# RWKV and DeltaNet scans with split state products, an mLSTM scan of 36 units in one line, and norm heads that add squares first

## What is computed

```python
h = rms_norm(x, g) * (1.0 + scale) + shift            # a "norm head", four of them
# DeltaNet, one chunk (RWKV is alike, with decays per channel):
delta = u_c - einsum('bhtk,bhvk->bhtv', w_c, s)        # u_c, w_c: triangular solve
o = einsum('bhtk,bhvk->bhtv', qd, s) + einsum('bhti,bhiv->bhtv', a_c, delta)
s = gl * s + einsum('bhtv,bhtk->bhvk', delta, kd)
# mLSTM, one chunk:
w_intra = exp(log_intra - m_t); w_inter = exp(log_inter - m_t)
s = einsum('bhtk,bhik->bhti', q, k) * w_intra
num = w_inter * einsum('bhtk,bhvk->bhtv', q, c) + einsum('bhti,bhiv->bhtv', s, v)
den = w_inter * einsum('bhtk,bhk->bht', q, n) + sum(s, axis=-1)
h = num / maximum(abs(den), exp(-m_t))
c = w_inter[-1] * c + einsum('bhi,bhiv,bhik->bhvk', w_end, v, k)
```

## Time and profile before

| | us |
|---|---|
| median of 3 runs (5168.05 to 5174.02) | 5173.57 |
| the profiled execution | 5176.75 |
| its span | 5175.1 |
| around the span | 1.65 |

### The profile page before, as it was taken

How to read it: one execution, slowest core, us unless ns; L and a number is a source line. 1 busy time by engine, 2 the same in 40 slices (tenths; PEclk the granted TensorE clock), 3 DMA queues, 4 the chain that set the end, 5 groups by cost and what they waited for, 6 DMA issues and landing times. The chain is left out here.

```text
span 5175.1 us, 94331 instructions
## 1 busy us (share of the span) xinstructions
PE 4152.8 (80%) x37921; PEld 3731.0 (72%) x37921; DVE 2183.8 (42%) x3966; ACT 1040.0 (20%) x1645; POOL 959.2 (19%) x676
## 2 busy tenths in 40 slices
PE   5999676367776778367999999799387388999998
PEld 3999332156665667156999999799366287999998
DVE  1333335233333434243655555200555435564555
ACT  2100223512222333222200010201222303110001
POOL 3322000000000422022222222321011023212222
PEclk8999888689999888678999999999566588999999
DMA  3222465311111211210111111122132311111111
GB/s 121 69 93 81 156 207 176 140 52 52 52 52 36 83 54 43 99 60 25 37 48 41 45 37 37 51 86 72 45 90 85 118 33 37 41 40 46 44 41 61
DMA packets 439441, 360.28 MB, mean 70 GB/s; under 512 B 63220, under 2 KB 417709, under 8 KB 436621
## 3 DMA queue, kind: packets, MB, share of 16 engines
q1 hardware_dynamic: 406993, 272.91, 17.6%
q0 software_dynamic: 10304, 60.98, 2.9%
q10 hardware_dynamic: 21888, 22.55, 1.2%
HBM read 270.45 MB, written 85.92 MB: 69 GB/s over the span
## 5 line engine op out<-in xcount | busy, mean ns | idle before, releaser
L91 POOL TENSOR_TENSOR ffn_w_lower<-ffn_w,ffn_w_upper 128x1024 fp32r<-128x1024 f32 x168 | 402.7, 2397 | 1296.0 <-DVE ffn_w_upper L86 1296.0
L872 DVE SCALAR_TENSOR_TENSOR conv_acc<-u_tile,ffn_taps,conv_acc 128x945 f32<-128x945 f32 (+3 forms) x440 | 488.9, 1111 | 86.9 <-ACT conv_acc L830 72.9
L99 PE MATMUL ffn_ps<-HU,ffn_w_upper 128*128 128x384 f32 x2112 | 485.7, 337 | 47.8 <-POOL HL L91 47.7
L99 PE MATMUL ffn_ps<-HU,ffn_w_lower 128*128 128x384 f32 x2112 | 484.0, 337 | 0.0
L99 PE MATMUL ffn_ps<-HL,ffn_w_upper 128*128 128x384 f32 x2112 | 483.7, 337 | 0.0
L99 PEld LDWEIGHTS ffn_ps<-HU,ffn_w_upper 128*128 128x128 f32 x2112 | 378.3, 189 | 55.3 <-POOL HL L91 33.5
L99 PEld LDWEIGHTS ffn_ps<-HU,ffn_w_lower 128*128 128x128 f32 x2112 | 380.6, 190 | 0.0
L99 PEld LDWEIGHTS ffn_ps<-HL,ffn_w_upper 128*128 128x128 f32 x2112 | 380.1, 190 | 0.0
L99 PE MATMUL ffn_out_ps<-g_upper,ffn_w_upper 128*128 128x384 f32 x1056 | 355.3, 336 | 14.4 <-DVE g_lower L91 14.4
L99 PE MATMUL ffn_out_ps<-g_lower,ffn_w_upper 128*128 128x384 f32 x1056 | 354.8, 336 | 0.0
L99 PE MATMUL ffn_out_ps<-g_upper,ffn_w_lower 128*128 128x384 f32 x1056 | 354.8, 336 | 0.0
(11 more groups left out here) (461 smaller groups left out, 6910.5 us busy)
## 6 DMA issues: line engine op xcount, KB each, us to landing
ffn_w<-in_ffn_w_in_dram SPq DMA_DIRECT2D x88, 512.0 KB
ada_w<-in_ada_w_dram SPq DMA_DIRECT2D x40, 1024.0 KB, 6.4
rwkv_units<-unit_rows POOLq DMA_DIRECT2D x8, 2304.0 KB, 8.9
un<-rwkv_units SPq DMA_DIRECT2D x36, 512.0 KB, 4.6
z_even<-z_tile POOLq DMA_DIRECT2D x31, 576.0 KB, 3.1
in_w<-in_ab_w_in_dram SPq DMA_DIRECT2D x31, 512.0 KB
gun<-gdn_units SPq DMA_DIRECT2D x72, 192.0 KB, 3.8
z_odd<-z_tile POOLq DMA_DIRECT2D x24, 576.0 KB, 4.9
```

What stands on the lines that cost most here:

```text
L91: return eng.tensor_tensor(out.bitcast(F32R), x, up, ALU.subtract)
L99: mm = pe.matmul(o, w(a).bitcast(F32R), r.bitcast(F32R), start=(first and n == 0), stop=(last and n == 2))
L872: dve.scalar_tensor_tensor(out=o, in0=i, scalar=tp[:, t:t + 1], in1=o, op0=ALU.mult, op1=ALU.add).then_inc(s["conv"] if n < NCONV else s[" ...
```

## The change

Four parts.

- **Norm heads.** VectorE adds the eight squares into one tile (`added`), then PE sums once with six matmuls. Squares and scaled blocks have four buffers in place of two; VectorE scales block k before it cuts block k-1. In `ffn_phase` the four buffers lie in the memory that the products use later.
- **RWKV scan.** The first product y0 (16 matmuls) opens the slot (`first`), then the products and the transposes of tokens and keys. VectorE makes the level 0 matrices before the masks. Update, both output products and the right side are made in halves, one between x and dy and one after dy of levels 1 to 5 (`beside`). ScalarE's output copy moves behind level 3. SyncE's loads wait for out_carried in place of out_own.
- **DeltaNet scan.** SyncE starts the output stores. A half of out stands ahead of dy in levels 1 and 2, a half of update in levels 3 and 4; state steps come in quarters in levels 4 and 5; the exponentials come one per level.
- **mLSTM scan.** Context and latent steps form one list of 36 units without a loop, with two state tiles (`ml_ctx`, `ml_lat`); states are turned in before the list and out after it. A constant `never` (a large negative number above the diagonal) is added on VectorE in place of clipping and GpSimd's mask, and ScalarE's exponential takes the column as its bias. The state product follows inter at once, in other columns of PSUM. GpSimd makes h, SyncE starts the stores, columns are read in place.

```diff
-        if k >= 2:
-            act.wait_ge(s["summed"], k - 1)
-        act.activation(self.tmp[k % 2], self.XT[:, k, :], ACT.Square).then_inc(s["squared"], 1)
-    act.wait_ge(s["summed"], KD)
+        if k > n:
+            act.wait_ge(s["added"], k - n)
...
 def tensor(self, pe):
-    for k in range(KD):
-        pe.wait_ge(self.s["squared"], k + 1)
-        for b, i, j in BANKS:
-            mm = pe.matmul(self.ps[:, b, 0:j - i], self.ones[:], self.tmp[k % 2][:, i:j],
-               start=(k == 0), stop=(k == KD - 1))
-        mm.then_inc(self.s["summed"], 1)
+    pe.wait_ge(self.s["added"], KD - 1)
+    for b, i, j in BANKS:
+        mm = pe.matmul(self.ps[:, b, 0:j - i], self.ones[:], self.rstd[:, i:j], start=True, stop=True)
...
+    s, n = self.s, len(self.tmp)
     dve.memset(self.eps[:], RMS_EPS).then_inc(s["eps_set"], 1)
+    for k in range(1, KD):
+        dve.wait_ge(s["squared"], k + 1)
+        if k > 1:
+            dve.wait_ge(s["added"], k - 1)
+        dve.tensor_tensor(self.rstd[:], self.rstd[:], self.tmp[(k - 1) % n], ALU.add).then_inc(s["added"], 1)
...
     for k in range(KD):
-        if k >= 2:
-            cut(k - 2)
-            dve.wait_ge(s["n_lower"], k - 1)
-        scale(k, self.tmp[k % 2])
-    cut(KD - 2)
+        if k >= n:
+            dve.wait_ge(s["n_lower"], k - n + 1)
+        for h, (a, b) in enumerate(HALVES):
+            dve.scalar_tensor_tensor(out=self.tmp[k % n][:, a:b], in0=self.XT[:, k, a:b], scalar=self.gain[:, k, h:h + 1],
+                         in1=self.rstd[:, a:b], op0=ALU.mult, op1=ALU.mult).then_inc(s["scaled"], 1)
+        if k:
+            cut(k - 1)
     cut(KD - 1)
...
+        def beside(l, g):
+            if l == 4:
+                if g == 0:
+                    rhs_carried(new)
+            elif l == 5:
+                rhs_own(new, g)
+            elif old is not None:
+                (update, out_carried, out_own)[l - 1](old, g)
+        if new is None:
+            solve(old)
+            for stage in (update, out_carried, out_own):
+                for g in range(2):
+                    stage(old, g)
+            return
+        first(new)
+        for g in range(2):
+            products(new, g)
+        tokens(new)
         if old is not None:
             solve(old)
-        if new is None:
-            update(old)
-            out_carried(old)
-            out_own(old)
-            return
-        tokens(new)
-        for g in range(2):
-            products(new, g)
         k_tokens(new)
         for g in range(2):
             dv.wait(pe, f"{a + g}n1", it)
-            block_w(pe, ps, st, K, B, a + g, g, 0)
-        if old is not None:
-            update(old)
         ac.wait(pe, f"{a}kt1", it)
         for l in range(1, NL - 1):
             each(block_w, l)
-            if l == 1 and old is not None:
-                out_carried(old)
-            if l == 4:
-                rhs_carried(new)
             each(block_x, l)
-            if l == 1 and old is not None:
-                out_own(old)
-            if l == 4:
-                rhs_own(new)
+            beside(l, 0)
             each(block_dy, l)
+            beside(l, 1)
         for g in range(2):
             dv.wait(pe, f"{a + g}Y{NL - 2}", it)
...
+        levels(1, 2, 3)
         if old is not None:
             out()
-        levels(3, 4)
+        levels(4, 5)
...
+                                         K["pairs0"][:, None, :, :].to_broadcast([P, 2, 2, RL]), ALU.mult), f"{a}Z{h}")
+            dv.wait(dve, f"{a}Z1", it)
+            for g in range(2):
+                dv.did(dve.tensor_tensor(Y[:, g], K["ident64"][:, None, :].to_broadcast([P, 4, RL]), W[:, g],
+                                         ALU.subtract), f"{a + g}Y0")
             for g in range(2):
                 q = a + g
...
+    def store(step):
+        it, a = step
+        to = [[o_dst[d, 2 * g + h, gdn_chunk(step, d)] for h, d in LANES] for g in range(2)]
+        early(sp, *to[0], *to[1])
+        for v in (pac.value(f"{a + g}yt", it) for g in range(2)):
+            sp.lower_val(v) if not isinstance(v, int) else None
+        for g in range(2):
+            pac.wait(sp, f"{a + g}yt", it)
+            for o, (h, d) in zip(to[g], LANES):
+                sp.dma_start(o, yt[:, g, h, d, :]).then_inc(stored[g], 16)
+    def turn(it, before_it):
+        for a in (0, 2):
+            load((it, a), True)
+            store((before_it, a))
     load((0, 0), False)
...
+                        (out if l <= 2 else update)(old, (l - 1) % 2)
                     for g in range(2):
...
             for g in range(2):
                 dv.wait(pe, f"{new[1] + g}qk", new[0])
-        level(1)
-        each(out, old)
-        level(2)
-        level(3)
-        each(update, old)
-        for l in range(4, NL):
+        if new is None:
+            each(out, old)
+            each(update, old)
+        for l in range(1, NL):
             level(l)
...
+        def output(g):
+            q = b + g
+            ppe.wait(act, f"{q}y", jt)
+            if not (isinstance(jt, int) and old == (0, 0)):
+                act.wait_ge(stored[g], number(old) * 64)
+            pac.did(act.activation(four(yt[:, g]), pq[:, g, :], ACT.Copy), f"{q}yt")
+        for l in range(1, NL):
+            levels(l)
+            if ahead is not None and l in (1, 2):
+                decay(ahead, l - 1)
+            if old is not None and l in (2, 3):
+                output(l - 2)
+            if ahead is not None and l in (4, 5):
+                growth(ahead, l - 4)
...
-        levels(0, 1, 2, 3, 4)
-        states(0)
-        states(1)
-        levels(5, 6)
+        half(block_dve, 0)
+        for l in range(1, NL):
+            half(block_dve, l)
+            if l in (4, 5):
+                states(l - 4, 0)
+            half(block_dve2, l)
+            if l in (4, 5):
+                states(l - 4, 1)
...
+                sp.dma_start(vv[:, q, h, d, :], z_src[8 + 2 * q + h, c]).then_inc(loaded[q], 16)
+    for q in range(4):
+        load(0, q)
+    for n, it, q, g in units:
+        if it < NCH - 1:
+            pe2.wait(sp, "num", n)
+            load(it + 1, q)
+        ph.wait(sp, "h", n)
+        for d in range(2):
+            sp.dma_start(hscan[d, chunk(it, d)][:, q * 256:q * 256 + 256],
+                         Ht[:, q, d].rearrange("p h v -> p (h v)")).then_inc(stored[q], 16)
+    for q in range(4):
...
+    def first(n, it, q, g):
+        if n >= 2:
+            dtail.wait(pe, "C", n - 2)
+        for i, (h, d) in enumerate(LANES):
+            c = chunk(it, d)
...
+    def second(n, it, q, g):
+        dintra.wait(pe, "s", n)
+        av.wait(pe, "v", n)
+        for h, d in LANES:
+            pe.matmul(ps[:, g, 2 + h, d * V1:d * V1 + V1], St[:, g, h, d, :], vt[:, g, h, d, :], start=True, stop=True)
+        if it > 1:
+            dtail.wait(pe, "C", n - 4)
+        for d in range(2):
+            for h in range(2):
+                pe.matmul(ps[:, g, h, d * V1:d * V1 + V1], kq[HALF[h], q, d, 1, :], state(it)[HALF[h], q, d, :],
+                          start=True, stop=True)
+        for d in range(2):
+            for h in range(2):
+                mm = pe.matmul(ps[HALF[h], g, d, 2 * V1:3 * V1], kt[:, g, h, d, :], vt[:, g, h, d, :],
+                               start=True, stop=True)
+        pe2.did(mm, "num")
+    for j in range(0, len(units), 2):
+        first(*units[j])
+        first(*units[j + 1])
+        second(*units[j])
+        second(*units[j + 1])
             @block.scalar
...
+    def intra(n, it, q, g):
+        dlog.wait(act, "w", n)
+        for h, d in LANES:
+            ins = act.activation(Wm[:, g, h, d, :], Wt[:, g, h, d, :], ACT.Exp,
+                                 bias=MC[:, chunk(it, d), 0, d, 2 * q + h:2 * q + h + 1])
...
+    def log(n, it, q, g):
+        pe1.wait(dve, "mb", n)
+        dlog.did(dve.tensor_tensor(four(Wt[:, g]), ps[:, g, 0, :], four(never[:]), ALU.add), "w")
...
+    for j in range(0, len(units), 2):
+        for stage in (log, intra, tail):
+            stage(*units[j])
+            stage(*units[j + 1])
             @block.gpsimd
...
+    for n, it, q, g in units:
+        dtail.wait(pool, "rec", n)
+        if it:
+            pool.wait_ge(stored[q], it * 32)
+        ph.did(pool.tensor_tensor(Ht[:, q].rearrange("p d h v -> p h d v"), NI[:, g, :, :, 0:P],
+                                  den[:, g, :, :, None].to_broadcast([P, 2, 2, P]), ALU.mult), "h")
...
         mlstm_prep_phase(nc, A, K, ztail2, mm_out)
-        zero_states_phase(nc, [ml_state[:]])
-        mlstm_scan_phase(nc, K, zc2, hscan, 1, ml_state)
+        zero_states_phase(nc, [ml_ctx[:]])
         with ExitStack() as t:
-            outs, ins = odd_states(nc, t, A, mc_out, mn_out, ml_state)
-            turn_states_phase(nc, K, outs, ins)
-        mlstm_scan_phase(nc, K, zc2, hscan, NCH - 1, ml_state)
```

(39 more changed lines are left out.)

459 lines of the change are left out of this document (174 added, 285 removed).

## The result

The changed kernel takes 5031.23 us (median of 4 runs, 5021.95 to 5041.01) against 5173.8 us before: a ratio of 0.972 with a 95% interval of 0.9702 to 0.9739. That is 143 us less; 5007 was forecast, 24 less than it became. Its profiled execution has a span of 5026.7 us, 148.4 less than that of the kernel before.

| stage | before us | after us | difference | forecast term |
|---|---|---|---|---|
| the four stages with a norm head (469.9, 886.2, 371.3, 886.0 before) | 2613.3 | 2627.6 | +14.3 | +22 |
| RWKV scan | 634.5 | 615.8 | -18.8 | -27 |
| DeltaNet scan | 398.9 | 342.1 | -56.9 | -52 |
| mLSTM from zeroing to the last state turn | 358.9 | 278.1 | -80.8 | -110 |
| everything else | | | -6 | 0 |

A forecast was written before the change was run, and what follows sets the result against it. PE, busy 4152.8 of 5175.1 us, was taken as the bound, losing time where it stands still or runs slowly. 5176.75 + 22 - 27 - 52 - 110 = 5010, less 3 to the median: 5007 us; range about 4960 to 5060, cold case 4950 to 5110.

The forecast's parts named there:

- Additions and GpSimd's share: Norm heads: seven VectorE additions at 1.40 us, plus 2.33 for one running beside a GpSimd instruction, ahead of PE's sum.
- nothing for the four buffers: Norm heads, second half: VectorE and GpSimd instructions run after each other, so the period stays 4.9 us; no gain.
- The rival with 2.3 us a block: Norm heads: four buffers work, GpSimd's 2.62 us becomes the period, -65 us, kernel 4942; chance 0.03.
- 1.5 us a slot, 27 in all: RWKV scan: semaphore waits fall from 3.5 to 2.0 us per slot over 18 slots, gaining 27 us.
- issue waits stay: RWKV scan: the 90 us of issue waits, read as code fetch, stay because a slot's code isn't shortened.
- The third rival: RWKV scan: code fetch eats the gain, kernel 5034 us; chance 0.06.
- the smaller waits: DeltaNet scan: 4 us gained from smaller waits, beside 24 for gXc and 10 for gW, 38 in all.
- I take the upper level: mLSTM: gaps under 1 us leave the clock high, so a pair takes 12.2 us and 18 pairs 220.
- zeroing, two state turns and the ends: mLSTM, around the list of units: 26 to 28 us together.
- The first rival: mLSTM: mixed clock, half its pairs cold, 15 us a pair, -61 us, kernel 5056; chance 0.20.
- The comparison with RWKV's 0.92: mLSTM: RWKV's stage with gaps of like size shows clock 0.92, so the upper level was expected.
- The rival on the slower side: mLSTM: 36 straight-line units pay code fetch stalls; at 5.3 us a unit the kernel takes 5198; chance 0.05.

The follow-up runs named there:

- ml_rows128: The changed kernel with the mLSTM's 8-row row product filled to 128 rows with zeros; 4976.3 us, ratio 0.9626 to the kernel before.
- ml_fill: The changed kernel with eight extra 128x128 transposes, read by nothing, after each mLSTM pair's second unit; 4974.5 us, ratio 0.9615 to the kernel before.

## Why the prediction was right or wrong

**The total.** The stages missed by +29 us (mLSTM), +8 (RWKV), -8 (norm heads), -5 (DeltaNet) and -6 (stages that the change doesn't touch). So the total came out nearer than its largest term, and that is luck.

**Norm heads: direction right (+14 for +22), two terms wrong that cancel in part, by luck.** Additions and GpSimd's share were forecast at 7x1.40 + 2.33 = 12.1 and took 12.1; the sum at 3.9 took 4.1. From the first square to the logarithm the four heads take 5.7, 6.6, 9.2 and 6.9 us longer than before, 28 together where 22 was forecast. What the step left out is the table load of 1.28, which the new order of two waits put behind the sum. The Trainium skill ("ScalarE: Activation LUTs", What ACT_TABLE_LOAD costs) gives about 1.28 us for a load and 1.38 for a drain with it; the trace has the same 1.28, and shows no drain: the load starts 0.08 us after the sum (2306.98 to 2307.06) and the logarithm 0.02 us after the load (2308.34 to 2308.36). The other failed term is "nothing for the four buffers": the period fell from 4.95 to 4.49, some 3 us a head, which the prediction itself had named as a sign of being wrong. VectorE's long scaling does stretch beside GpSimd (the pair of pieces takes 3.9 in place of 1.55), as argued from the earlier trace rows, but the first, small piece now runs before GpSimd starts. The rival with 2.3 us a block was five times too big.

**RWKV: the semaphore waits right, the gain not.** 1.5 us a slot, 27 in all, was the forecast for semaphore waits; they fell by 26.7 (62 to 35.3), with the wait for the keys' copy at 0.95 where 0.8 was forecast. The step that failed is "issue waits stay": they rose by 38 us. The stage fell by 19 all the same because PE's busy time fell by 27, and that the rows don't explain: the number of matmuls is the same. The prediction read issue waits as code being fetched; no run shows what they are. The third rival is right in part: more of the gain came back as issue waits.

**DeltaNet: total right (57 for 52), in part by luck.** The waits for gXc and gW fell by 24 and 11 us as the sum had them (24 and 10). But where it took 4 more from the smaller waits, those rose by 11, above all PE's waits for gY and gX, so all semaphore waits fell by 24 in place of 38. That was made up by terms put too low: PE's busy time fell by 23, where the sum had 14 (nine pieces at half of 3.68 would be 16.6), and issue waits by 9, where it had nothing. The clock rose from 0.88 to 0.92 as forecast. And the 24 for gXc are not the stores' move alone: with the stores put back that wait is 11.6, and the stage 11 to 22 us longer.

**mLSTM: the term of the sum that was mis-sized, 110 for 81.** The step is "PE would work 10.7 of 12.2 us with gaps under 1 us ...: I take the upper level". The gaps were as forecast (0.88), the chain too: at the upper clock it takes 11.05 us a pair, a little less than the 12.2 of the working, and that kernel's scan 210.7 us where 220 was forecast. The clock was not: 0.74, and 14.5 us a pair in place of 12.2 are 41 us over 18 pairs. A second term hid 10 of them: zeroing, two state turns and the ends took 17.4 us (278.1 less 260.7) where 28 was put. The first rival, a mixed clock at 15 us a pair, is what happened (14.5), with the difference that not every second pair but half of every pair is slow. The comparison with RWKV's 0.92 looked at gaps alone. All matmuls of the RWKV scan have 64 or 128 rows; the mLSTM has a product of 8 rows twice a pair, and ml_rows128 shows that filling it up takes the clock to 0.97 with the gaps left as they are. The rule of the Trainium skill weighed there ("TensorE: Matmul & The Clock Gate", Part 4: PE-mode transpose, by which transposes don't engage the full clock) would have kept the scan cold for another reason; the runs disagree with it: ml_rows128 has all its transposes and runs at 0.97, and ml_fill reached 0.94 by adding transposes.

**The rival on the slower side** had 36 units in one line pay for code. PE's list of waits for that stage has no issue wait at all. One difference to the RWKV scan is that matmuls come less densely (1656 in 261 us; RWKV has 14760 in 616); no run tests whether that is the reason.

## What to carry to other kernels

Where a stage shows a low granted clock while PE is busy, look for matmuls that use few rows and try filling them with zeros before reordering anything; here the product took the same 1.16 us. A faster engine may be worth nothing until the chain through the others is shorter (nothing before, 50 us after): measure both together before dropping either. Where issue waits are large, semaphore waits taken away can come back as issue waits, as in the RWKV scan; count on less than the sum. A stage that an edit doesn't touch can move by 10 to 20 us, so judge a small gain by the touched stage and by the total.

## What the runs showed of the hardware

- With eight matmuls of 8 rows twice per pair the clock of the mLSTM scan was 0.74 with PE busy 91% of the time, and 0.71 in another order with PE busy 95%; with 120 rows of zeros added on both sides of the same matmuls it was 0.97 and 0.95.
- With the 8 rows left and eight more transposes per pair it was 0.94. With the full rows in the kernel before, where PE waits up to 3.9 us at a time, it was 0.72.
- A stand-still of 0.88 us in every 11 us left the clock at 0.97.
- ScalarE's table load stands behind or ahead of a wait depending on which of two waits comes first; it is 1.28 us each time.
- The RWKV scan, with the same instructions, took 609.5 to 631.4 us in programs that differ only in other stages; the DeltaNet scan 332.6 to 342.8.
